# Split values as the stationary side in three attention branches, and a new order of branch C, of the start and of the last projection

## The chip, the core and the metric

The kernel runs as one program on one core of a Trainium2 chip. TensorE (PE in the profile) multiplies 128x128 blocks: a weight load (PEld) puts a stationary block into the array, and a matmul streams moving columns past it into PSUM. VectorE (DVE), ScalarE (ACT) and GpSimd (POOL) work element by element. Each engine runs its own list of instructions in order, and engines wait for each other by semaphores. The metric is device microseconds of one launch, the median of the runs.

## What is computed

Two layers, each a set of five attention branches (four heads each, 512 tokens, model width 1024) with gates, an output projection and a layer norm:

```python
def hybrid_layer(x, mem, ...):
    pr = split_projection(x @ w_in)
    o_a = dsa_attention(aq, ak, av, iq, ik, pr['i_w'])     # top 128 keys of each query, by index scores
    o_b = moba_attention(bq, bk, bv)                       # block-sparse, causal
    o_c = diff_attention(cq, ck, cv, lam)                  # (softmax1 - lam * softmax2) v
    o_d = mla_attention(qn, qr, kn, kr, v)                 # 96-wide keys from latents
    o_e = memory_attention(eq, mk, mv)                     # 256 memory tokens
    # each o_*: times silu(z), @ w_branch, times sigmoid(g); summed; @ w_out
    return layer_norm(alpha * x + out)

def mla_attention(qn, qr, kn, kr, v):
    s = (einsum('bqhd,bkhd->bhqk', qnb, kn) + einsum('bqhr,bkr->bhqk', qrb, kr)) * scale
    p = softmax(where(causal, s, -inf))
    return einsum('bhqk,bkhd->bqhd', p, v)
```

## The kernel before

**Products.** Each large product is made of three passes over operands split in a head and a rest (`product3`: head by head, head by rest, rest by head). The weights come by DMA in units (`WEIGHTS`): SyncE loads a unit, ACT copies its head (`split`, L1031), POOL subtracts for the rest (L721), and PE uses it in groups. A group `("grp", c, u, t)` is unit u of chunk c for token tile t: six matmuls with 512 moving columns (296 in chunk IX). A gate chunk (`gE0`, ...) has a fifth group per unit, t = 4, that projects a branch's output into bank U.

**The plan.** `plan()` writes one list, `PLAN`, for all engines: the groups in order, and after each group the smaller steps that `spread` puts between two places (`PLACES`) in equal shares of the groups' width. Every engine walks the same list, does its part of each step, and skips the rest. So what stands early in the list is early on every engine.

**Attention of A, B, D and E** (`att_steps`). Unit u = 4j + t is head j, query tile t, with (t + 1) x 128 keys (256 in E). Its steps are S (scores on PE into bank S; the mask and the row maximum on DVE, L1412; the exponential on ACT, L1114), two units later T (PE transposes the probabilities into bank TP, L962; ACT copies them to `PT`, L1120), and one more unit later V (PE, L977): f32 matmuls with a 128x128 block of `PT` stationary and 64 columns of values moving, t + 1 of them. Bank TP is free for the next T when ACT has copied it. After a head's last V, `fo` and `fin` (DVE) divide by the row sums and multiply by the gate z, and `yj` transposes the result and splits it for the branch's projection. `ev` and `er` copy and split the transposed queries and keys of a head (ACT, DVE) before its scores.

**Branch C** (`diff_steps`) has two score maps per unit; W (DVE, L1464 to L1467) joins them before T. Its keys and queries stand in the product banks G2 and G3, and its steps lie between (gA0,0,0) and (D0,3,2). W stands one half step before T, and `ev` of a map does queries and keys in one step.

**Start and end.** At the start the residual's four token tiles are normed (`ln0`), transposed and split (`xj`); the first groups go through units 0 and 1 of chunk IX, tile by tile. At the end of a layer chunk O1 runs units 0 and 1 over all tiles and then units 2 and 3 in pairs, tile by tile; `l1` and `l2` norm a finished tile (DVE, ACT, then POOL L677, then the store), and stand at the last groups.

## Time and profile before

| | us |
|---|---|
| median of 3 runs | 1382.11 |
| lowest and highest | 1380.39, 1382.39 |
| the profiled execution | 1384.15 |
| its span (first to last instruction) | 1382.5 |
| PE busy in it | 1328.0 (96%) |
| weight loads (PEld) busy | 1130.7 (82%) |
| DVE, ACT, POOL busy | 661.8, 653.3, 669.9 (48%, 47%, 48%) |

Busy time is a union of overlapping instructions, so a PE that is always busy may still be set by the pace of its matmuls. That pace is read from the starts of neighbouring rows in the timeline. A mean duration of a matmul is longer than its share of the engine.

### The profile page before, as it was taken

Reading aid. Unit: us, or ns where it says so; the run is one execution under the profiler, and the core shown is the slowest. Engines: PE = TensorE matmul, PEld = TensorE weight load, DVE = VectorE, ACT = ScalarE, POOL = GpSimd, SP = SyncE. Lnnn points to the kernel's source line nnn. Section 1 sums busy time; section 2 is a strip of 40 time slices with the busy share of each in tenths; the row PEclk is TensorE's granted clock in tenths of the full one; section 3 lists DMA queues with packets and bytes.
Section 4 is the critical chain, followed back from the end, with each engine's and each line's share of the span. In section 5 each row is a group of like instructions: output and inputs, shape, how many; then the busy total and the mean of one; then the engine's idle time right before and its main releaser. Section 6 shows DMA issues by size and latency. Waiting matters only on the chain.

```text
span 1382.5 us, 19021 instructions
## 1 busy us (share of the span) xinstructions
PE 1328.0 (96%) x6872; PEld 1130.7 (82%) x6872; DVE 661.8 (48%) x1609; ACT 653.3 (47%) x1296; POOL 669.9 (48%) x850
## 2 busy tenths in 40 slices
PE   6999999999988999999999999999999899999995
PEld 5888878888877898888888888888888779888884
DVE  4646696433155753213265668753322665432044
ACT  4455345454275664423245543555434665643232
POOL 3543453255563444467464435334446434645764
PEclk9899999999998999999999999999999999999998
DMA  7322242231331143232413223223123213323221
GB/s 258 114 77 62 81 114 58 67 88 47 103 95 37 37 123 107 58 107 77 140 49 106 68 71 106 81 58 85 53 74 111 59 33 86 95 65 100 84 77 61
DMA packets 147052, 116.47 MB, mean 84 GB/s; under 512 B 5520, under 2 KB 131856, under 8 KB 146704
## 3 DMA queue, kind: packets, MB, share of 16 engines
q1 hardware_dynamic: 146816, 114.22, 27.8%
q8 instruction: 55, 0.90, 0.3%
q10 hardware_dynamic: 144, 1.05, 0.2%
q14 instruction: 37, 0.30, 0.1%
HBM read 112.10 MB, written 3.15 MB: 83 GB/s over the span
## 4 chain that ended last, share of the span: by engine, by line
PE 79%; DVE 12%; ACT 4%; issue 2%; POOL 1%; DMA 1%; SPq 0%; POOLq 0%; DVEq 0%; ACTq 0%
PE product L737 19%; PE product L738 18%; PE product L739 18%; PE context L977 5%; PE scores L949 3%; PE transposed L962 3%; PE branch_product L737 2%; PE branch_product L739 2%; PE branch_product L738 2%; DVE index_scores L1389 2%; DVE top_eight L1395 1%; DMA residual<-in_x_dram 1%; ACT score_operands L1001 1%; POOL residual L677 1%; DVE vector_scratch L1214 1%
## 5 line engine op out<-in xcount | busy, mean ns | idle before, releaser
L721 POOL TENSOR_TENSOR weights_rest<-raw_weights,weights_head 128x320 fp32r<-128x320 f32 (+3 forms) x672 | 540.1, 836 | 376.8 <-ACT weights_head L1001 376.8
L737 PE MATMUL product<-weights_head,stationary_head 128*128 128x512 f32 (+3 forms) x768 | 291.4, 379 | 7.8 <-POOL weights_rest L721 7.6
L1001 ACT ACTIVATE weights_head<-raw_weights 128x1280 fp32r<-128x1280 f32 (+4 forms) x178 | 198.3, 1115 | 200.3 <-PE product L739 153.5
L739 PE MATMUL product<-weights_head,stationary_rest 128*128 128x512 f32 (+3 forms) x768 | 285.6, 372 | 0.0
L738 PE MATMUL product<-weights_rest,stationary_head 128*128 128x512 f32 (+3 forms) x768 | 285.4, 372 | 0.0
L737 PE MATMUL product<-stationary_head,weights_head 128*128 128x512 f32 x640 | 263.5, 412 | 0.0
L738 PE MATMUL product<-stationary_rest,weights_head 128*128 128x512 f32 x640 | 252.6, 395 | 0.0
L739 PE MATMUL product<-stationary_head,weights_rest 128*128 128x512 f32 x640 | 252.1, 394 | 0.0
L704 POOL TENSOR_TENSOR merged<-merged,activated 128x256 f32<-128x256 f32 x128 | 93.0, 748 | 291.4 <-DVE activated L1533 291.2
L737 PEld LDWEIGHTS product<-weights_head,stationary_head 128*128 128x128 f32 x768 | 145.7, 190 | 29.8 <-POOL weights_rest L721 8.4
L739 PEld LDWEIGHTS product<-weights_head,stationary_rest 128*128 128x128 f32 x768 | 145.4, 189 | 23.7
L738 PEld LDWEIGHTS product<-weights_rest,stationary_head 128*128 128x128 f32 x768 | 145.9, 190 | 20.2
L1114 ACT ACTIVATE probabilities<-probabilities,negated_maxima 128x256 f32<-128x256 f32 (+3 forms) x160 | 86.3, 540 | 155.4 <-DVE negated_maxima L1412 154.4
L739 PEld LDWEIGHTS product<-stationary_head,weights_rest 128*128 128x128 f32 x640 | 121.5, 190 | 27.5
L737 PEld LDWEIGHTS product<-stationary_head,weights_head 128*128 128x128 f32 x640 | 121.8, 190 | 20.8
L738 PEld LDWEIGHTS product<-stationary_rest,weights_head 128*128 128x128 f32 x640 | 122.1, 191 | 19.3
L1533 DVE SCALAR_TENSOR_TENSOR activated<-activated,branch_product 128x512 f32<-128x512 f32 x64 | 44.0, 687 | 154.5 <-PE branch_product L739 149.6
L1412 DVE CUSTOM_DVE_ANT_0 probabilities<-scores,consts_sb 128x256 f32<-128x256 f32 (+3 forms) x136 | 60.4, 444 | 110.8 <-PE scores L949 110.6
L1175 ACT ACTIVATE activated<-product 128x512 f32<-128x512 f32 x80 | 47.7, 596 | 131.4 <-PE product L739 130.5
L977 PEld LDWEIGHTS context<-values_and_gates,probabilities_T 128*128 128x128 f32 x640 | 89.8, 190 | 9.9 <-issue 1.4
L1001 ACT ACTIVATE probabilities_T<-transposed 128x256 f32<-128x256 f32 (+3 forms) x160 | 67.2, 420 | 55.3 <-PE transposed L962 54.0
L949 PE MATMUL scores<-score_operands 128*128 128x256 f32 (+7 forms) x288 | 77.7, 324 | 10.3 <-DVE score_operands L1350 6.1
(200 smaller groups left out, 1812.5 us busy)
## 6 DMA issues: line engine op xcount, KB each, us to landing
raw_weights<-in_w_in_dram SPq DMA_DIRECT2D x104, 512.0 KB, 3.7
raw_weights<-in_w_in_dram SPq DMA_DIRECT2D x72, 256.0 KB, 2.9
raw_weights<-in_w_branch_dram SPq DMA_DIRECT2D x80, 128.0 KB, 3.7
raw_weights<-in_w_out_dram SPq DMA_DIRECT2D x16, 512.0 KB, 3.6
merged<-in_w_mem_kv_dram SPq DMA_DIRECT2D x8, 512.0 KB, 7.3
raw_weights<-in_w_in_dram SPq DMA_DIRECT2D x8, 416.0 KB, 3.1
raw_weights<-in_w_in_dram SPq DMA_DIRECT2D x8, 296.0 KB, 3.8
residual<-in_x_dram SPq DMA_DIRECT2D x4, 512.0 KB, 11.4
```

The source lines that it names most:

```text
L704: ins = nc.gpsimd.tensor_tensor(m[:, part], m[:, part], TH[:, s, part], ALU.add)
L721: ins = nc.gpsimd.tensor_tensor(WL[:, sw, part], RAW[:, sr, part], WH[:, sw, part].bitcast(F32), ALU.subtract)
L737: nc.tensor.matmul(dst, sh, mh, start=start, stop=False)
L738: nc.tensor.matmul(dst, sh, ml, start=False, stop=False)
L739: return nc.tensor.matmul(dst, sl, mh, start=False, stop=stop)
L949: last = nc.tensor.matmul(S[:, 0:w], lhs, rhs, start=i == 0, stop=i == len(passes) - 1)
L977: last = nc.tensor.matmul(O[:, 0:BW][:, t * HD:(t + 1) * HD], PT[:, i * P:(i + 1) * P], v, start=i == 0, stop=i == w // P - 1)
L1001: return nc.scalar.activation(dst, src, ACT.Copy, scale=scale)
L1114: nc.scalar.activation(p, p, ACT.Exp, bias=NMX[:, m:m + 1], scale=-1.0, accum_out=RS[:, j % 2, 2 * t + u % 2 if b == "C" else t:(2 * t + u ...
L1175: nc.scalar.activation(TH[:, s, :], G[u % 2][:], ACT.Tanh, scale=0.5).then_inc(act_out.sem, act_out.step((c, u)))
L1412: nc.vector.tensor_tensor_reduce(probs(b, u)[:, 0:w], S[:, 0:w], bias, -SCALE[b], -TAKEN, ALU.add, ALU.min, NMX[:, u % 4:u % 4 + 1]).then_ ...
L1533: nc.vector.scalar_tensor_tensor(out=TH[:, s, :], in0=TH[:, s, :], scalar=1.0, in1=U[:], op0=ALU.add, op1=ALU.mult).then_inc(used.sem, not ...
```

## The change

Three things change together.

**Branches A, B and D** (`WIDE`). ACT copies the transposed probabilities as a head (fp32r, now a step of T), and a new step `pr` subtracts on DVE for the rest; both hold two query tiles side by side. A step `vs` splits a head's values into one 128-column block, head beside rest. V now exists for odd units alone: the split values are stationary, and 256 or 128 columns of probabilities move, head and rest, four matmuls for t = 1 and eight for t = 3. The output stands transposed in bank O, its two halves are added (`fo` on ACT, `fa` on DVE), and the gate z is divided by the row sums (`fin`), transposed (`zj`) and multiplied in. Bank TP is free only when `pr` is done.

**Branch C** starts at (C1,0,2), with its first head's queries and keys in banks U and O, and ends at (D0,3,1). W stands two half steps before T; `ev` and `er` handle one operand each.

**Start and end.** In chunk IX tiles 0 and 1 go through units 0 to 2 first. The splits of units 0 and 1 stand before the work on tile 3, the split of unit 2 behind it, and tile 3 of the input is loaded later. In chunk O1 each tile is finished in turn, and `l1`, `l2` of a tile stand one or two groups behind it. The early split of the next layer's first unit (`ahead`) goes.

```diff
+WIDE = "ABD"
...
+def wide_steps(b):
+    if b == "D":
+        out = [[("qt", b, 0)], [("ev", b, 0)], [("er", b, 0), ("qt", b, 1)], [("ev", b, 1)], [("er", b, 1)], [("vs", b, 0)]]
+    else:
+        out = [[("qt", b, 0)], [("ev", b, 0), ("er", b, 0)], [("ev", b, 1), ("er", b, 1)], [("vs", b, 0)]]
+    for i in range(UNITS + LAG_V + 1):
+        first, second = [], []
+        u = i - LAG_V
+        if 0 <= u < UNITS and u % 2 == 1:
+            first.append(("V", b, u))
+        if u >= NT and u % NT == 0:
+            first.append(("fa", b, u // NT - 1))
+        if 0 <= i - LAG_T < UNITS:
+            first.append(("T", b, i - LAG_T))
+            second.append(("pr", b, i - LAG_T))
+        if i < UNITS:
+            second.append(("S", b, i))
+        if i in (4, 8):
+            second += prep_steps(b, 1 + i // 4)
+        if i in (5, 9):
+            first.append(("er", b, 1 + i // 4))
+        if 0 <= u < UNITS and u % NT == NT - 1:
+            j = u // NT
+            second += [("fo", b, j)] + ([("vs", b, j + 1)] if j + 1 < NH else []) + [("fin", b, j)]
+        if i == 12:
+            second.append(("zj", b, 0))
+        if u == UNITS:
+            second.append(("zj", b, 1))
+        out += [first, second]
+    return out
...
 def diff_steps():
-    out = [[("qt", "C", 0)], [("ev", "C", 0, 0)], [("er", "C", 0, 0), ("ev", "C", 0, 1)], [("er", "C", 0, 1)], []]
-    late = []
+    out = [[("qt", "C", 0)]] + [[] for _ in range(5)]
+    early = {}
+    for j in range(NH):
+        for n in range(4):
+            m, part = divmod(n, 2)
+            at = {0: n - 5, 1: n}.get(j, 2 * (4 * j - 3) + 1 + n)
+            early.setdefault(at, []).append(("ev", "C", j, m, part))
+            early.setdefault(at + 1, []).insert(0, ("er", "C", j, m, part))
+    for n in range(5):
+        out[1 + n] += early.get(n - 5, [])
     for i in range(UNITS + 3):
-        first, second, third = [], [], []
+        first, second = [], []
         if 0 <= i - 3 < UNITS:
             first.append(("V", "C", i - 3))
+            if (i - 3) % NT == NT - 1:
+                first.append(("fo", "C", (i - 3) // NT))
+                second.append(("fin", "C", (i - 3) // NT))
         if 0 <= i - 2 < UNITS:
             first.append(("T", "C", i - 2))
         if i < UNITS:
             first.append(("S", "C", 2 * i))
-            second.append(("S", "C", 2 * i + 1))
+            second.insert(0, ("S", "C", 2 * i + 1))
         if 0 <= i - 1 < UNITS:
-            second.insert(0, ("W", i - 1))
-        second += late
-        late = []
-        if i >= 3 and (i - 3) % NT == NT - 1:
-            first.insert(1, ("fo", "C", (i - 3) // NT))
-            third.append(("fin", "C", (i - 3) // NT))
+            first.append(("W", i - 1))
         if i == 4:
-            third.append(("qt", "C", 1))
-        j, m = divmod(i + 3, 4)
-        if j < NH and m < 2 and i < UNITS:
-            third.append(("ev", "C", j, m))
-            late = [("er", "C", j, m)]
-        out += [first, second + third]
+            second.append(("qt", "C", 1))
+        out += [first + early.get(2 * i, []), second + early.get(2 * i + 1, [])]
...
-    ("lambda", ("gB1", 3, 3), ("C0", 0, 2), 0.0),
-    ("C attention", ("gA0", 0, 0), ("D0", 3, 2), 0.0),
+    ("lambda", ("gB0", 2, 0), ("gB0", 2, 0), 0.0),
+    ("C attention", ("C1", 0, 2), ("D0", 3, 1), 0.0),
...
-        pairs = {"IX": (0,), "O1": (2,)}.get(c, ())
-        for u in range(units(c)):
-            if u in pairs:
-                groups += [(c, u + i, t) for t in range(NT) for i in range(2)]
-            elif u - 1 not in pairs:
-                groups += [(c, u, t) for t in range(parts(c))]
+        order = [(u, t) for u in range(units(c)) for t in range(parts(c))]
+        if c == "IX":
+            order = [(u, t) for t in range(2) for u in range(3)] + [(u, t) for u in range(3) for t in (2, 3)] + [(3, t) for t in range(NT)]
+        elif c == "O1":
+            order = [(0, t) for t in range(NT)] + [(1, 0), (1, 1), (2, 0), (3, 0), (2, 1), (3, 1)] + [(u, t) for t in (2, 3) for u in range(1, 4)]
+        groups += [(c, u, t) for u, t in order]
...
-    start = [("ln0", 0), ("ln0", 1), ("mkv", 0), ("ln0", 2), ("xj", 0, 0), ("xj", 0, 1), ("ln0", 3), splits[0], ("mkv", 1),
-             ("xj", 1, 0), ("xj", 1, 1), ("ln0", 4), splits[1], splits[2]]
...
+    start = [("ln0", 0), ("ln0", 1), ("mkv", 0), ("ln0", 2), ("xj", 0, 0), ("xj", 0, 1), splits[0], splits[1], ("mkv", 1),
+             ("xj", 1, 0), ("xj", 1, 1), ("ln0", 3), splits[2], ("ln0", 4)]
+    extra[at[(ORDER[0], 1, 1)]] += [("xj", 2, 0), ("xj", 2, 1)]
+    extra[at[(ORDER[0], 2, 1)]] += [("xj", 3, 0), ("xj", 3, 1)]
...
-    extra[at[("O1", 2, 1)]] += [("ahead",) + WEIGHTS[0]]
-    extra[at[("O1", 3, 1)]] += [("l1", 0)]
-    extra[at[("O1", 3, 2)]] += [("l1", 1), ("l2", 0)]
-    extra[at[("O1", 3, 3)]] += [("l1", 2), ("l2", 1), ("l1", 3), ("l2", 2), ("l2", 3)]
+    for t in range(NT - 1):
+        i, j = {0: (("O1", 2, 1), ("O1", 3, 1))}.get(t, (("O1", 1, t + 1), ("O1", 2, t + 1)))
+        extra[at[i]].append(("l1", t))
+        extra[at[j]].append(("l2", t))
+    extra[at[("O1", 3, 3)]] += [("l1", 3), ("l2", 3)]
...
+        def wide(b):
+            if b == "D":
+                ph, pl = KLZ[:].rearrange("p a n -> p (a n)"), PL[:]
+            else:
+                ph, pl = (TL[:, a:a + 2, :].rearrange("p a n -> p (a n)") for a in (4, 6))
+            return [x.rearrange("p (i n) -> p i n", i=NT) for x in (ph, pl)] + [TL[:, 8, :].rearrange("p (i c d) -> p i c d", i=NT, c=2)]
+        def y_rows(k):
+            return PT if k == 0 else DS
...
-            load_x(3)
             load_mk(0, 3)
             for L in range(DEPTH):
                 new_layer([*raw, ln_in], L)
                 for i, item in enumerate(LOADS):
+                    if L == 0 and i == 2:
+                        load_x(3)
...
-                        freed["TP"] = (moved, L, step)
+                        freed["TP"] = (rest, L, ("pr", b, u)) if b in WIDE else (moved, L, step)
+                    elif kind == "V" and step[1] in WIDE:
+                        _, b, u = step
+                        j, t = divmod(u, NT)
+                        ph, pl, vs = wide(b)
+                        if t == 1:
+                            claim("O")
+                            pe.wait_ge(rest.sem, rest.at(L, ("vs", b, j)))
+                        pe.wait_ge(rest.sem, rest.at(L, ("pr", b, u)))
+                        blocks = [(0, ph), (t, ph), (t, pl)] + [(i, p) for i in range(1, t) for p in (ph, pl)]
+                        blocks.insert(3 if t == 1 else 1, (0, pl))
+                        for n, (i, p) in enumerate(blocks):
+                            at = P if i == t else 0
+                            last = nc.tensor.matmul(O[:, (t - 1) * P + at:(t + 1) * P], vs[:, i].rearrange("p c d -> p (c d)"),
+                                                    p[:, i, at:2 * P], start=n == 0, stop=n == len(blocks) - 1)
+                        last.then_inc(v_done.sem, v_done.step((b, u)))
+                        if t == NT - 1:
+                            freed["O"] = (summed, L, (b, j))
...
+                    elif kind == "vs":
+                        _, b, j = step
+                        if j > 0:
+                            act.wait_ge(v_done.sem, v_done.at(L, (b, NT * j - 1)))
+                        else:
+                            act.wait_ge(copied.sem, copied.at(L, ("dk" if b == "D" else b + "1", NT - 1)))
+                        copy(wide(b)[2][:, :, j % 2, :], VZ[:, vz(b), :, j * HD:(j + 1) * HD]).then_inc(moved.sem, moved.step(step))
+                    elif kind == "fo" and step[1] in WIDE:
+                        _, b, j = step
+                        r, o = rows(j)
+                        act.wait_ge(v_done.sem, v_done.at(L, (b, NT * j + NT - 1)))
+                        copy(y_rows(j // 2)[r, :], O[o, :]).then_inc(moved.sem, moved.step(step))
...
-                        copy(PT[:, 0:w], TP[:, 0:w]).then_inc(moved.sem, moved.step(step))
+                        if b in WIDE:
+                            half = slice(t % 2 * P, (t % 2 + 1) * P)
+                            copy(wide(b)[0][:, 0:t + 1, half], TP[:, 0:w].rearrange("p (i n) -> p i n", n=P)).then_inc(moved.sem, moved.step(step))
+                        else:
+                            copy(PT[:, 0:w], TP[:, 0:w]).then_inc(moved.sem, moved.step(step))
...
+                    elif kind == "vs":
+                        _, b, j = step
+                        v, vs = VZ[:, vz(b), :, j * HD:(j + 1) * HD], wide(b)[2]
+                        dve.wait_ge(moved.sem, moved.at(L, step))
+                        nc.vector.tensor_tensor(vs[:, :, 1 - j % 2, :], v, vs[:, :, j % 2, :].bitcast(F32),
+                                                ALU.subtract).then_inc(rest.sem, note(rest, step))
+                    elif kind == "pr":
+                        _, b, u = step
+                        t, _, w = unit(b, u)
+                        ph, pl, _ = wide(b)
+                        half = slice(t % 2 * P, (t % 2 + 1) * P)
+                        dve.wait_ge(moved.sem, moved.at(L, ("T", b, u)))
+                        nc.vector.tensor_tensor(pl[:, 0:t + 1, half], TP[:, 0:w].rearrange("p (i n) -> p i n", n=P),
+                                                ph[:, 0:t + 1, half].bitcast(F32), ALU.subtract).then_inc(rest.sem, note(rest, step))
+                    elif kind == "fa":
+                        _, b, j = step
+                        r, _ = rows(j)
+                        y = y_rows(j // 2)
+                        dve.wait_ge(moved.sem, moved.at(L, ("fo", b, j)))
+                        nc.vector.tensor_tensor(y[r, :], O[r, :], y[r, :], ALU.add).then_inc(summed.sem, note(summed, (b, j)))
...
```

On PE, in branch B's first head, the rows are the transposed probabilities (L962, L1030), the context products of the last query tile (L977, L1047) and the scores. Before:

```order
L949 MATMUL scores<-key_rests,score_operands 128x128
L977 MATMUL context<-values_and_gates,probabilities_T 128x64 x3
L962 MATMUL transposed<-consts_sb,probabilities 128x128 x4
L737 MATMUL product<-stationary_head,weights_head 128x512
```

Now:

```order
L1017 MATMUL scores<-key_rests,score_operands 128x256
L793 MATMUL product<-stationary_head,weights_head 128x512
...
L1047 MATMUL context<-score_operands 128x256 x2
L1047 MATMUL context<-score_operands 128x128 x2
L1047 MATMUL context<-score_operands 128x256 x4
L1030 MATMUL transposed<-consts_sb,probabilities 128x128
```

Before, each unit has its context product (three f32 matmuls here, each of which is two records in the trace). Now eight fp32r matmuls serve the two units t = 2 and t = 3.

On DVE, in branch C's first head, the rows are the mask and maximum of a score map (L1412, L1562), the joining of two maps (L1464 to L1467, L1614 to L1617) and the rests of the operands (L1348, L1350, L1501). Before:

```order
L1412 ISA index_scores,negated_maxima<-scores,consts_sb 128x512
L1412 ISA negated_maxima 128x1
L1533 SCALAR_TENSOR_TENSOR activated<-activated,branch_product 128x512
L1464 RECIPROCAL map_factors<-row_sums 128x1
L1465 SCALAR_TENSOR_TENSOR map_factors<-map_factors,lambdas,row_sums 128x1
L1467 SCALAR_TENSOR_TENSOR probabilities<-probabilities,map_factors 128x384
L1412 ISA index_scores,negated_maxima<-scores,consts_sb 128x512
```

Now:

```order
L1562 ISA index_scores,negated_maxima<-scores,consts_sb 128x512
L1562 ISA negated_maxima 128x1
L1614 RECIPROCAL map_factors<-row_sums 128x1
L1615 SCALAR_TENSOR_TENSOR map_factors<-map_factors,lambdas,row_sums 128x1
L1617 SCALAR_TENSOR_TENSOR probabilities<-probabilities,map_factors 128x384
L1683 SCALAR_TENSOR_TENSOR activated<-activated,branch_product 128x512
L1562 ISA index_scores,negated_maxima<-scores,consts_sb 128x512
```

The joining of unit 2 now stands ahead of the gate's multiplication (L1683), and directly behind the first mask of the unit after it.

On DVE, at the end of the program, the rows are the last tiles' residual, statistics and norm. Before:

```order
L1540 SCALAR_TENSOR_TENSOR residual<-product,residual 128x512
L1226 BN_STATS half_tile_stats<-residual 128x6
L1231 BN_AGGR norm_stats<-half_tile_stats 128x2
L1236 RECIPROCAL norm_stats<-deviations 128x1
L1237 SCALAR_TENSOR_TENSOR norm_stats<-norm_stats 128x1
L1243 TENSOR_TENSOR residual<-residual,values_and_gates 128x1024
L1283 SCALAR_TENSOR_TENSOR residual<-residual,norm_stats,values_and_gates 128x1024
L1243 TENSOR_TENSOR residual<-residual,values_and_gates 128x1024
L1292 RECIPROCAL norm_stats<-deviations 128x1
L1295 SCALAR_TENSOR_TENSOR residual<-residual,norm_stats,values_and_gates 128x512 x2
```

Now:

```order
L1351 TENSOR_TENSOR residual<-residual,values_and_gates 128x1024
L1690 SCALAR_TENSOR_TENSOR residual<-product,residual 128x512
L1334 BN_STATS half_tile_stats<-residual 128x6
L1339 BN_AGGR norm_stats<-half_tile_stats 128x2
L1391 SCALAR_TENSOR_TENSOR residual<-residual,norm_stats,values_and_gates 128x1024
L1400 RECIPROCAL norm_stats<-deviations 128x1
L1403 SCALAR_TENSOR_TENSOR residual<-residual,norm_stats,values_and_gates 128x512 x2
```

The two gains of earlier tiles (L1243) that stood behind the last tile's residual now stand ahead of it.

## Rows read from the trace of the kernel before

**Rows 1.** The page, part 1: busy us, share of the span, instructions.
```profile
PE 1328.0 (96%) x6872; PEld 1130.7 (82%) x6872; DVE 661.8 (48%) x1609; ACT 653.3 (47%) x1296; POOL 669.9 (48%) x850
```
**Rows 2.** Busy time by stretch: stretch, its length, engines, PEclk, DMA share, GB/s.
```profile
205.00:275.00 70.00, 68.76 (x385) 59.28 (x386) 39.65 (x99) 36.12 (x76) 23.38 (x28) 1.00 0.22 62
...
395.00:490.00 95.00, 86.94 (x443) 74.46 (x442) 57.04 (x148) 54.75 (x126) 40.09 (x51) 0.95 0.15 43
530.00:590.00 60.00, 60.00 (x344) 52.08 (x343) 17.41 (x49) 29.03 (x62) 27.66 (x35) 1.00 0.29 84
...
1068.00:1160.00 92.00, 83.90 (x428) 71.46 (x427) 56.49 (x146) 53.40 (x121) 38.71 (x49) 0.96 0.16 45
```
**Rows 3.** The waits of PE: total us, times, longest.
```profile
PE transposed L962 <- DVE probabilities L1467: 8.8, 10, 1.8
PE product L737 <- POOL weights_rest L721: 7.6, 3, 4.1
PE scores L949 <- DVE score_operands L1350: 6.1, 4, 1.5
```
**Rows 4.** The timeline of PE in branch A: start, duration, engine, line, names, count.
```profile
322.91 1.08 PEld L977 LDWEIGHTS context<-values_and_gates,probabilities_T 128*128 128x128 f32 x8
323.14 1.00 PE L977 MATMUL context<-values_and_gates,probabilities_T 128*128 128x64 f32 x8
...
323.97 0.28 PE L962 MATMUL transposed<-consts_sb,probabilities 128*128 128x128 f32 x1
```
**Rows 5.** The same, fp32r score matmuls of 256 and 128 columns in A and B.
```profile
321.52 0.28 PE L949 MATMUL scores<-score_operands 128*128 128x256 f32 x1
...
321.75 0.40 PE L737 MATMUL product<-stationary_head,weights_head 128*128 128x512 f32 x1
...
230.48 0.22 PE L949 MATMUL scores<-score_operands 128*128 128x128 f32 x1
...
230.66 0.83 PE L977 MATMUL context<-values_and_gates,probabilities_T 128*128 128x64 f32 x6
```
**Rows 6.** DVE, groups by line and shape: count, busy us, mean ns, idle before.
```profile
L1308 DVE TENSOR_TENSOR stationary_rest<-transposed,stationary_head 128x512 fp32r<-128x512 f32 x8 | 5.5, 690 | 19.8 <-ACT stationary_head L1001 19.8
```
**Rows 7.** The timeline of branch B: ACT's copy of the probabilities, and V.
```profile
233.55 0.60 ACT L1001 ACTIVATE probabilities_T<-transposed 128x512 f32<-128x512 f32 x1
...
234.78 1.00 PE L977 MATMUL context<-values_and_gates,probabilities_T 128*128 128x64 f32 x8
```
**Rows 8.** The timeline of branch C: DVE's joining and PE's wait.
```profile
412.27 1.05 DVE L1467 SCALAR_TENSOR_TENSOR probabilities<-probabilities,map_factors 128x384 f32<-128x384 f32 x1
...
413.46 0.52 PE L962 MATMUL transposed<-consts_sb,probabilities 128*128 128x128 f32 x3 [1.78 <-DVE probabilities L1467]
```
**Rows 9.** The timeline of the start.
```profile
26.01 1.28 DVE L1226 BATCH_NORM_STATS2 half_tile_stats<-residual 128x6 f32<-128x512 f32 x2
...
28.34 0.60 PE L856 MATMUL context<-consts_sb,residual 128*128 128x128 f32 x4
...
28.70 2.77 POOL L677 TENSOR_TENSOR residual<-residual,values_and_gates 128x256 f32<-128x256 f32 x4 [3.65 <-DVE residual L1243]
...
31.42 1.58 POOL L721 TENSOR_TENSOR weights_rest<-raw_weights,weights_head 128x320 fp32r<-128x320 f32 x2
...
33.06 0.61 PE L737 MATMUL product<-weights_head,stationary_head 128*128 128x296 f32 x1 [4.12 <-POOL weights_rest L721]
```
**Rows 10.** DVE's gains from 1357 us to the end, grouped by shape.
```profile
L1243 DVE TENSOR_TENSOR residual<-residual,values_and_gates 128x1024 f32<-128x1024 f32 x3 | 4.2, 1390 | 0.0
```
**Rows 11.** The timeline of the end.
```profile
1365.67 0.68 DVE L1540 SCALAR_TENSOR_TENSOR residual<-product,residual 128x512 f32<-128x512 f32 x1
1365.84 12.12 POOL L677 TENSOR_TENSOR residual<-residual,values_and_gates 128x256 f32<-128x256 f32 x12 [12.68 <-DVE residual L1243]
...
1372.51 2.15 DVE L1295 SCALAR_TENSOR_TENSOR residual<-residual,norm_stats,values_and_gates 128x512 f32<-128x512 f32 x2
...
1378.37 1.26 SPq L664 DMA_DIRECT2D out_dram<-residual  x2
```

133 lines of the change are left out of this document (85 added, 48 removed).

## The prediction

> **What bounds the kernel now.** I read the busy shares first: PE is busy for 1328.0 of 1382.5 us [rows 1]. Then the stretches, to see whether a full PE hides slack. In the stretch of branch D (530 to 590) PE is busy for all 60.00 us while DVE works 17.41 and ACT 29.03; in that of branch B 68.76 of 70.00, with DVE at 39.65. In the two stretches of branch C it is 86.94 of 95.00 and 83.90 of 92.00, and there the granted clock is 0.95 and 0.96 [rows 2]. Last the waits: most of what PE waits for is DVE in branch C (joined maps 8.8 us, rests of score operands 6.1 us) and POOL at the start (7.6 us) [rows 3]. So outside C and the two ends only less work on PE helps, inside C only shorter waits.
>
> **V of A, B and D.** In a head V was 1 + 2 + 3 + 4 = 10 f32 matmuls, and each stands as two records with a weight load of its own: four of them are eight records, and from their start to the next transpose are 0.83 us, so 0.104 us a record [rows 4]. A head costs 20 x 0.104 = 2.08 us. Now it is twelve fp32r matmuls, eight with 256 and four with 128 moving columns. The nearest rows are the score matmuls: two with 256 columns take 321.52 to 321.75, 0.115 us each; two with 128 take 230.48 to 230.66, 0.09 us each [rows 5]. That is 8 x 0.115 + 4 x 0.09 = 1.28 us. The difference is 0.80 us a head, for 4 heads, 3 branches and 2 layers 24 x 0.80 = 19.2 us. If a 128-column matmul costs a full 0.115 us, it is 16.8 us. All of it lies on PE in stretches where PE never rests, so I take 19.
>
> These eight records have one weight load each, 1.08 us in all, and start at the pace of the loads [rows 4]. The Trainium skill (FP8 and Floating Point Precision, section TensorE Precision Notes) says that true FP32 is four passes through the array. Priced by passed columns alone, an old block would be 4 x 64 columns and a head 2560, as many as the new twelve matmuls have, and the gain would be nothing. The trace speaks against pricing by columns here, since the loads set the pace.
>
> **What the new steps put beside it.** Per unit there is one subtraction on DVE from a PSUM bank. A 512-column one of that kind takes 0.69 us [rows 6]. PE's V now waits for ACT's copy and this, and the next T for it too, since the bank TP is held longer. In branch B the copy ends at 233.55 + 0.60 = 234.15 and V starts at 234.78 [rows 7]: a margin of 0.63 us, which 0.69 us and the queue of top-eight operations in front of it use up. In D (and in A, by the starts around 323 us) DVE has 40 us in 60 free [rows 2] and the plan leaves about the same two half steps, so I expect nothing there. In B some five odd units a layer are as tight; at 0.4 us each, both layers, that is 4 us. Bounds: 0 where the queue is empty, 12 us where one top-eight operation over 512 columns (about 0.7 us, taken as the 512-column row of [rows 6]) stands in front of each of the 16 V. The head's ends (`vs`, `fo`, `fa`, `zj`) have four half steps, some 6 us, until the next V or the projection wants them, and ACT and DVE need 0.6 + 0.7 us for each pair: nothing. With this cover gone each would cost its 1.3 us.
>
> **Branch C.** Idle PE in its stretches is 8.06 and 8.10 us; the reduced clock takes 0.05 x 95 = 4.8 and 0.04 x 92 = 3.7 us of full speed [rows 2]. The pool is 24.6 us. The waits come from W one half step before T: at 413.46 PE had waited 1.78 us, W ended at 412.27 + 1.05 = 413.32 [rows 8], and it had stood behind a gate multiplication. Now W stands two half steps before T and ahead of that multiplication, and the branch is spread over 68 groups where it had 55, so a half step grows from 1.28 to 1.55 groups: some 2.1 us of PE work where it was 1.75. From the last exponential W needs 1.7 to 2 us, and now has over 4. The rests of the keys come in four steps of one operand, each a half step apart, and end one half step before the scores. DVE has 57 us of work in 95, in the longer stretch about half. Late next is the first scores' key rest of each head, with one half step for 0.7 us. I take 22 of the 24.6 us, the clock's part with the waits', because it fell only beside them. Bounds: 11 (the waits halve, and the clock stays) and 25.
>
> **The end.** From the last tile's residual at 1365.67 to the end of its norm at 1372.51 + 2.15 = 1374.66 are 9.0 us [rows 11], and two gains of 1.39 us [rows 10] stand in it; both now lie before. One of them is still running when the last residual is ready, which costs 0.8 us. The norm ends at 1365.67 + 0.8 + 9.0 - 2.8 = 1372.7. Today the last stores wait until 1378.37, behind POOL's twelve pieces of 12.12 us [rows 11]. POOL now starts tile 2 at about 1366.4 and needs four pieces of 1.01 us, till 1370.5, with tiles 0 and 1 done before. So the stores follow at once, and 4.1 us after their issue the span ends, as now: 1376.9 instead of 1382.5, 5.6 us. Bounds 4 and 7. The split of unit 3 of O1 has three groups of 1.36 us less 0.1 us to spare: nothing.
>
> **The start.** Today PE waits 4.12 us for the first rest of weights, at 33.06 [rows 9]. The first split moves ahead of tile 3, so PE starts as its transposes end, about 29. But unit 2 is now wanted third, and its split stands behind tile 3, whose statistics stand on DVE behind the copies of tile 1: they begin at about 30, not at 26.01. From these statistics to POOL's first split are today 31.42 - 26.01 = 5.4 us, and the split takes 1.58 us [rows 9], so unit 2 is ready at 30.2 + 5.4 + 1.6 = 37.2, when PE has two groups done, as it has today at 37.5. The loads of tile 3 and of the weights change places under this. POOL's pieces may lengthen beside DVE's wide operations, so I take a loss of 1 us; bounds a gain of 3 and a loss of 4. In the second layer the same order costs and saves under 1 us.
>
> **The sum.** 19 + 22 + 5.6 - 4 - 1 = 41.6 us. The span goes from 1382.5 to 1340.9, the profiled execution from 1384.15 to 1342.6, which was 2 us above the median: the median goes from 1382.1 to 1340.5, so 1341.
>
> **Rivals.** 1. *DVE is late in B*: the twelve-microsecond bound is met, and small waits stand in A and D as well, 4 more. For it: the margin of 0.63 us; against it: B's DVE is free for 30 us in 70. It gives 1341 + 8 + 4 = 1353. Chance 0.16.
> 2. *C keeps half of its waits*, the clock with them: 1341 + 11 = 1352. For it: the operands of a head still end one half step before its scores. Chance 0.10.
> 3. *The V matmuls are no cheaper*, paced by the columns passed: 1341 + 19 = 1360. Against it are [rows 4, 5]. Chance 0.02. It is the case that the Trainium skill's rule above would give.
> 4. *A shared port.* POOL's pieces of 256 columns take 2.77 / 4 = 0.69 us at 28.70 and 12.12 / 12 = 1.01 us at the end [rows 9, 11], where wide DVE operations on two SBUF operands run beside them. The change adds such operations: 24 of `vs` at some 0.4 us and 12 splits of the branch output at 0.69, 18 us in all. If POOL's splits of weights stood still for them and PE felt a third, it would be 1341 + 6 = 1347. The Trainium skill (SBUF — State Buffer, section SBUF: two separate sides) states such a lock of the port that GpSimd shares with VectorE. Chance 0.04.
> 5. *All goes well*: no wait in B, a start that gains: 1341 - 4 - 4 = 1333. Chance 0.08.
> 6. *Slower*: the transposes wait for `pr` in every unit. There are 24 heads with four T and two V, 144 places, so 41.6 us are eaten at 0.29 us each. In B alone (48 places) one top-eight operation in front costs 34 us; if PE's clock in B then falls to the 0.9 to 0.95 that C has now, 140 us of B lose 7 to 14 us more, and with C's gain halved too, the kernel is at 1341 + 34 + 12 + 11 = 1398. It needs DVE full in B, which has 57% now and some 75% by my count after. Chance 0.04.
>
> The forecast itself, 1333 to 1349, has 0.56. The range must leave out no more than 2 in 10: 1329 to 1355, which takes in cases 1, 2, 4 and 5. About 0.2% is what a measurement can tell from no change: faster 0.95, same 0.01, slower 0.04.
>
> **What would show it.** In the profile after: context rows of A, B and D with 128x256 and 128x128 shapes and starts 0.115 and 0.09 us apart; no DVE joining among PE's waits, and a clock of 1.00 in C's stretches; a new wait of PE for DVE's rest of the probabilities in B, 2 to 6 us a layer, and near none in A and D; a wait of 4 to 6 us for POOL at about 32 us; last stores some 7 us after PE's last product. The forecast is wrong if the waits for that rest pass 12 us, or if the clock is below 1.00 in C or B.

## The result, and the profile after

| | before | changed |
|---|---|---|
| median, us | 1381.25 | 1422.38 |
| lowest and highest | 1379.29, 1382.39 | 1421.56, 1424.71 |
| span of the profiled execution | 1382.5 | 1423.1 |

The changed kernel takes 1.0302 times as long (95% interval 1.0283 to 1.0321): 41 us more, where 41 us less were forecast. The page's part 1, answering [rows 1]:

```profile
PE 1327.7 (93%) x6680; PEld 1115.5 (78%) x6680; DVE 735.9 (52%) x1741; ACT 673.9 (47%) x1344; POOL 673.8 (47%) x850
```

PE has 192 records fewer, 24 heads with twelve in the place of twenty, and DVE has 74 us more work. The waits of PE (total us, times, longest), answering [rows 3]:

```profile
PE context L1047 <- DVE score_operands L1435: 29.1, 21, 3.5
PE branch_product L949 <- DVE score_operands L1481: 11.7, 2, 5.9
PE product L793 <- POOL weights_rest L777: 10.4, 2, 8.9
PE scores L1017 <- DVE score_operands L1501: 6.7, 4, 1.9
PE context L1047 <- DVE probabilities_T_rest L1435: 6.4, 8, 1.1
PE scores L1017 <- DVE negated_maxima L1562: 6.4, 10, 2.1
```

The joining of the maps (8.8 us in [rows 3]) is gone. In its place stand 35.5 us of V waiting for `pr` (L1435, both of its rows), and two waits of 5.9 us for L1481, which is `ek`. Busy time in the stretches of B, A, C, D and of C in the second layer (columns as in [rows 2]):

```profile
203.00:290.00 87.00, 76.58 (x374) 62.65 (x373) 60.08 (x143) 40.35 (x83) 27.32 (x32) 0.94 0.22 60
290.00:370.00 80.00, 74.86 (x388) 61.51 (x387) 40.02 (x90) 42.43 (x87) 37.96 (x47) 1.00 0.23 67
416.00:515.00 99.00, 93.42 (x490) 81.46 (x491) 57.98 (x155) 57.10 (x132) 46.41 (x59) 0.98 0.19 56
536.00:620.00 84.00, 80.38 (x428) 66.77 (x427) 36.30 (x95) 41.16 (x86) 37.19 (x46) 1.00 0.30 86
1109.00:1209.00 100.00, 94.34 (x494) 82.01 (x493) 58.90 (x159) 57.48 (x134) 46.65 (x59) 0.98 0.20 56
```

B, which had 68.76 of 70.00 at a clock of 1.00 in [rows 2], has 76.58 of 87.00 at 0.94: it has become what C was. The same products run in both kernels, so their starts cut the two traces into like pieces. Each row is the time from the first product of one chunk to that of the next one named, layer 0 and layer 1, in us. The piece that begins with gE1 holds B's last three heads, and C's steps lie inside the piece that begins with C0:

| piece | before | changed | difference |
|---|---|---|---|
| start, up to A1 | 79.1 | 91.6 | +12.5 |
| A1 to gE1 (E, first head of B) | 146.0, 146.0 | 145.4, 145.5 | -0.6, -0.5 |
| gE1 to gB0 (rest of B) | 40.1, 40.1 | 53.5, 53.5 | +13.4, +13.4 |
| gB0 to C0 (A) | 75.7, 75.6 | 79.7, 79.6 | +4.0, +4.0 |
| C0 to gC0 (C) | 172.7, 171.8 | 166.0, 166.0 | -6.7, -5.8 |
| gC0 to gD0 (D) | 81.0, 81.0 | 83.4, 83.4 | +2.4, +2.4 |
| gD0 to O1 | 76.7, 76.7 | 76.2, 76.2 | -0.5, -0.5 |
| O1 to A1 of layer 1 | 80.9 | 89.3 | +8.4 |
| last O1 to the end | 39.0 | 33.9 | -5.1 |

So the three changed V cost 37.5 us (B, A, D and the two small pieces), the start and the layer's boundary 20.9, branch C gives 12.5 and the end 5.1.

**Where V waits.** The timeline of B at the end of its first head (start, duration, engine, line; idle time before and its releaser in brackets), PE:

```profile
232.04 1.20 PE L1047 MATMUL context<-score_operands 128*128 128x256 f32 x8 [0.17 <-DVE score_operands L1435]
233.08 0.27 PE L1030 MATMUL transposed<-consts_sb,probabilities 128*128 128x128 f32 x1
...
234.57 0.33 PE L1017 MATMUL scores<-score_operands 128*128 128x384 f32 x1
...
240.87 0.70 PE L1047 MATMUL context<-score_operands 128*128 128x256 f32 x4 [2.35 <-DVE score_operands L1435]
```

ACT: exponential (L1218), the output's copy `fo`, the values' copy of `vs`, and the copy of T:

```profile
235.71 0.62 ACT L1218 ACTIVATE probabilities<-probabilities,negated_maxima 128x384 f32<-128x384 f32 x1 [0.29 <-DVE negated_maxima L1562]
...
236.44 0.59 ACT L1088 ACTIVATE probabilities_T<-context 64x512 f32<-64x512 f32 x1
236.94 0.41 ACT L1088 ACTIVATE score_operands<-values_and_gates 128x256 fp32r<-128x256 f32 x1
237.37 0.38 ACT L1088 ACTIVATE score_operands<-transposed 128x256 fp32r<-128x256 f32 x1
```

DVE: `vs`, the division (`fin`), `fa`, a round of the top-eight selection, the gate's multiplication, and last `pr`:

```profile
237.38 0.42 DVE L1427 TENSOR_TENSOR score_operands<-values_and_gates,score_operands 128x256 fp32r<-128x256 f32 x1 [1.71 <-ACT score_operands L1088]
...
238.12 0.42 DVE L1460 TENSOR_TENSOR values_and_gates<-values_and_gates,reciprocals 128x256 f32<-128x256 f32 x1
238.47 0.67 DVE L1442 TENSOR_TENSOR probabilities_T<-context,probabilities_T 64x512 f32<-64x512 f32 x1
...
239.13 0.67 DVE L1539 MATCH_REPLACE8 index_scores<-top_eight,index_scores 128x512 f32<-128x512 f32 x1
239.73 0.67 DVE L1680 SCALAR_TENSOR_TENSOR merged<-activated,branch_product 128x512 f32<-128x512 f32 x1
240.32 0.41 DVE L1435 TENSOR_TENSOR score_operands<-transposed,score_operands 128x256 fp32r<-128x256 f32 x1
```

V of the first head was done at 233.08, but ACT reached the copies only after an exponential that had to wait for later scores. The copy of T, which `pr` reads, stood behind them too. DVE stood idle for 1.71 us, with five operations of 0.4 to 0.7 us (and two short ones) still to do before `pr`. The next two heads begin with waits of 3.46 and 2.38 us. In A the same places show 1.11, 2.11 and 1.19 us.

**The start.** PE, POOL and DVE:

```profile
40.77 0.61 PE L793 MATMUL product<-weights_head,stationary_head 128*128 128x296 f32 x1 [8.91 <-POOL weights_rest L777]
...
34.46 2.77 POOL L735 TENSOR_TENSOR residual<-residual,values_and_gates 128x256 f32<-128x256 f32 x4 [7.00 <-DVE residual L1351]
37.18 3.54 POOL L777 TENSOR_TENSOR weights_rest<-raw_weights,weights_head 128x320 fp32r<-128x320 f32 x2
...
31.77 1.28 DVE L1334 BATCH_NORM_STATS2 half_tile_stats<-residual 128x6 f32<-128x512 f32 x2
...
36.51 1.80 DVE L1351 TENSOR_TENSOR residual<-residual,values_and_gates 128x1024 f32<-128x1024 f32 x1 [1.31 <-ACT residual L1097]
38.34 1.76 DVE L1372 TENSOR_TENSOR residual<-residual,values_and_gates 128x1024 f32<-128x1024 f32 x1
```

PE has done two groups when it stands for 8.91 us. Some 27 us later, in chunk E, PE and DVE again:

```profile
67.59 0.42 PE L949 MATMUL branch_product<-consts_sb,merged 128*96 128x128 f32 x1 [5.86 <-DVE score_operands L1481]
67.67 0.78 PE L793 MATMUL product<-weights_head,stationary_head 128*128 128x512 f32 x1
...
55.90 0.64 DVE L1320 TENSOR_TENSOR vector_scratch<-staged_features,consts_sb 128x36 f32<-128x36 f32 x1 [6.04 <-ACT staged_features L1088]
...
64.49 1.41 DVE L1476 MEMSET score_operands<- 64x256 f32 x4
...
66.25 0.42 DVE L1481 TENSOR_TENSOR score_operands<-branch_product,score_operands 64x256 fp32r<-64x256 f32 x1
```

The first index transpose needs bank U, which holds memory keys until `ek` has read them. The change put `ek` behind (IX, 3, 1), and so behind the rotations of tiles 0 and 1 (L1320 to L1656), which keep DVE from 55.90 to 64.49. After the wait the granted clock is 0.50 from 67.6 to 72.0 (products of 0.63 to 0.78 us where 0.39 is usual). The second layer has the same wait, 5.86 us at 761.66.

### The profile page after: what moved, and what is told of

The parts are those of the page before. It is cut to its first block, busy times and chain, and to the rows that moved or that the text cites. A ratio compares the mean times of both kernels' runs of the same rounds, so it can differ in the third digit from the quotient of the medians.

```text
span 1423.1 us, 18843 instructions
## 1 busy us (share of the span) xinstructions
PE 1327.7 (93%) x6680; PEld 1115.5 (78%) x6680; DVE 735.9 (52%) x1741; ACT 673.9 (47%) x1344; POOL 673.8 (47%) x850
## 4 chain that ended last, share of the span: by engine, by line
PE 68%; DVE 20%; ACT 7%; issue 3%; POOL 1%; DMA 0%; DVEq 0%; ACTq 0%; SPq 0%
PE product L793 16%; PE product L795 16%; PE product L794 16%; PE context L1047 3%; PE scores L1017 2%; PE branch_product L793 2%; PE branch_product L795 2%; PE branch_product L794 2%; PE transposed L1030 2%; ACT score_operands L1088 2%; DVE index_scores L1539 2%; DVE probabilities L1562 2%; PE context L1064 1%; DVE top_eight L1545 1%; ACT probabilities L1218 1%
## 5 line engine op out<-in xcount | busy, mean ns | idle before, releaser
L777 POOL TENSOR_TENSOR weights_rest<-raw_weights,weights_head 128x320 fp32r<-128x320 f32 (+3 forms) x672 | 547.1, 845 | 414.0 <-ACT weights_head L1088 413.7
L1218 ACT ACTIVATE probabilities<-probabilities,negated_maxima 128x256 f32<-128x256 f32 (+3 forms) x160 | 86.6, 541 | 192.8 <-DVE negated_maxima L1562 190.8
L1683 DVE SCALAR_TENSOR_TENSOR activated<-activated,branch_product 128x512 f32<-128x512 f32 x64 | 43.9, 686 | 132.5 <-PE branch_product L795 128.4
L1562 DVE CUSTOM_DVE_ANT_0 probabilities<-scores,consts_sb 128x256 f32<-128x256 f32 (+3 forms) x136 | 60.0, 442 | 49.3 <-PE scores L1017 49.0
L1017 PEld LDWEIGHTS scores<-score_operands 96*128 96x128 f32 (+1 forms) x288 | 52.5, 190 | 28.1 <-DVE negated_maxima L1562 19.7
L793 PE MATMUL branch_product<-branch_out_T_head,weights_head 128*128 128x512 f32 x160 | 66.1, 413 | 0.0
```

What stands on the lines that cost most here:

```text
L777: ins = nc.gpsimd.tensor_tensor(WL[:, sw, part], RAW[:, sr, part], WH[:, sw, part].bitcast(F32), ALU.subtract)
L793: nc.tensor.matmul(dst, sh, mh, start=start, stop=False)
L1017: last = nc.tensor.matmul(S[:, 0:w], lhs, rhs, start=i == 0, stop=i == len(passes) - 1)
L1218: nc.scalar.activation(p, p, ACT.Exp, bias=NMX[:, m:m + 1], scale=-1.0, accum_out=RS[:, j % 2, 2 * t + u % 2 if b == "C" else t:(2 * t + u ...
L1562: nc.vector.tensor_tensor_reduce(probs(b, u)[:, 0:w], S[:, 0:w], bias, -SCALE[b], -TAKEN, ALU.add, ALU.min, NMX[:, u % 4:u % 4 + 1]).then_ ...
L1683: nc.vector.scalar_tensor_tensor(out=TH[:, s, :], in0=TH[:, s, :], scalar=1.0, in1=U[:], op0=ALU.add, op1=ALU.mult).then_inc(used.sem, not ...
```

## The experiments

Each is an edit of the changed kernel; medians are compared with 1422.4 us of the changed kernel and with the kernel before, run beside each (1381.6 to 1381.9).

**Old V.**

```diff
-WIDE = "ABD"
+WIDE = ""
```

> The changed kernel with the old V in A, B and D (branch C, the start and the end stay changed). Theory, read from the starts of the same product groups in the two traces: after the change B's stretch is 12.9 and 13.0 us longer, A's 4.0 and 3.9, D's 1.8 and 1.8, so the new V costs 37.4 us of 1422.4 and this kernel takes 1385, 4 us more than before. Rival 1: the loss sits in the other two parts, and V brings its gain: then this kernel is at or above 1422. Rival 2: taking V back also gives the clock and the queues of C and the start room: below 1378.

Measured: 1388.57 us (ratio to before 1.0054, 1.0039 to 1.0069). The new V costs 34 us. B's, A's and D's pieces are again 40.1, 75.7 and 81.0 us, as before to 0.1 us; the start, the boundary and C stay within 1.1 us of the changed kernel's. Neither rival stands. The median is 3.6 us above the sum; the profiled span, 1386.7, is 1.0 us above what the pieces give (1423.1 - 37.4).

**`ek` early.**

```diff
-    extra[at[(ORDER[0], 3, 1)]].append(("ek",))
+    extra[at[(ORDER[0], 1, 2)]].append(("ek",))
```

> The changed kernel with one step moved: ek (copies of the memory keys out of banks U and S, on ACT and DVE) stands behind group (IX, 1, 2), the ninth of the chunk's sixteen, and no longer behind (IX, 3, 1), where it stood behind the rotations of two tiles on DVE. Theory: PE's two waits of 5.86 us for line L1481 (at 67.6 and 761.7 us) go, and with each some 2 us of half clock behind it: 8.2 + 7.7 = 15.9 us less, 1406 to 1408. Rival: PE then waits nearly as long for the index transposes' own data, since the rotations themselves are late: at most 4 us less, 1418 or more.

Measured: 1406.88 us, 15.5 less. Both waits for L1481 are gone, and the pieces up to A1 are 83.5 us (91.6) and 82.2 us (89.3). The rival falls.

**Old start.**

```diff
-            order = [(u, t) for t in range(2) for u in range(3)] + [(u, t) for u in range(3) for t in (2, 3)] + [(3, t) for t in range(NT)]
+            order = [(u, t) for t in range(NT) for u in range(2)] + [(u, t) for u in (2, 3) for t in range(NT)]
...
-                    if L == 0 and i == 2:
-                        load_x(3)
```

with `splits`, `xj`, `ek` and the load of tile 3 where they were.

> The changed kernel with the start of before: the order of chunk IX's groups, the places of the splits, of xj and ek, and of the load of input tile 3 (the early split of the next layer stays away). Theory: the start's stretch up to chunk A1 is 12.5 us longer than before, and that of the second layer 8.4; all of it comes back, 1401.5. If ek alone is the cause (the run with ek early), this is within 5 us of that run. Rival: without the early split the second layer waits for it and keeps 4 us or more of its loss: 1405 or more.

Measured: 1404.14 us, between the theory (1401.5) and its rival (1405 or more). The start takes 77.3 us, 1.8 less than before, and the piece across the boundary 82.9 us (80.9 before, 89.3 changed): the second layer keeps 2 us, not the rival's 4. Whether they are the missing early split or the new order of O1, no run tells. Most of the loss of the start and boundary was `ek`. In layer 0 the new order of groups, splits and loads cost 83.5 - 77.3 = 6.2 us beside it, or 83.5 - 79.1 = 4.4 against the kernel before; no run tells where the 1.8 us between these two come from.

**The split of unit 2 ahead of tile 3**, with `ek` early:

```diff
-             ("xj", 1, 0), ("xj", 1, 1), ("ln0", 3), splits[2], ("ln0", 4)]
+             ("xj", 1, 0), ("xj", 1, 1), splits[2], ("ln0", 3), ("ln0", 4)]
```

> The kernel with ek early (1406.9 us), and the split of unit 2 of chunk IX ahead of the work on input tile 3. Theory: POOL's 3.5 us split at 37.18 us, which PE awaited for 8.9 us, is done before 29; the wait and the half clock behind it go, though PE then waits 2 to 3 us for tile 3: 6 to 8 us less, 1399 to 1401. Rival: tile 3 is what bounds the start in either order: at most 2 us less, 1405 or more.

Measured: 1403.42 us (1399.90 to 1404.21), 3.5 less by the medians, which is less than the theory asked for. In the profiled execution, the fastest of the four, the start takes 76.8 us, 6.7 less than with `ek` early alone and 2.3 less than before. Beside the run with the old start (77.3) the new order of groups is then worth 0.5 us: no loss, and hardly a gain. The two POOL pieces of this split:

```profile
31.54 1.57 POOL L777 TENSOR_TENSOR weights_rest<-raw_weights,weights_head 128x320 fp32r<-128x320 f32 x2 [4.32 <-ACT weights_head L1088]
```

In the changed kernel the same two pieces took 3.54 us, beside DVE's two additions over 128x1024.

**A second buffer for the split values**, in A and B, with `vs` behind the first V of the head before:

```diff
-                        if j > 0:
-                            act.wait_ge(v_done.sem, v_done.at(L, (b, NT * j - 1)))
+                        if j > 0 and b == "D":
+                            act.wait_ge(v_done.sem, v_done.at(L, (b, NT * j - 1)))
+                        elif j > 1:
+                            act.wait_ge(v_done.sem, v_done.at(L, (b, NT * (j - 1) - 1)))
...
+        if b != "D" and u % NT == 1 and 0 <= u < UNITS - NT:
+            second.append(("vs", b, u // NT + 1))
```

Heads 1 and 3 use `PL`, which is free outside D.

> The changed kernel with two buffers for the split values of A and B: the split of a head's values stands right behind the first V of the head before, and waits for no output. D is as changed. Theory (head of line): at a head's end DVE stood idle 1.7 us for ACT's copy of the values, which stands behind an exponential and the copy of the output, and pr of the next head stood behind that; PE's waits at the first V of heads 1 to 3 (2.35, 3.46 and 2.38 us in B, 1.11, 2.11 and 1.19 in A, each layer) fall to a third, and the half clock behind two of them in B goes: 20 us less or more, 1402 or less. Rival (DVE is full: top-eight, gate and mask in front of pr): DVE is only filled in another order, at most 5 us less, 1417 or more.

Measured: 1413.59 us, 8.8 less: between the two theories. The waits at the first V of a head became smaller, but new ones stand at the second V, where `vs` now stood ahead of `pr`, with a clock fall behind the largest:

```profile
239.34 0.70 PE L1049 MATMUL context<-score_operands,probabilities_T_rest 128*128 128x256 f32 x4 [0.96 <-DVE score_operands L1439]
248.37 2.08 PE L1049 MATMUL context<-score_operands,probabilities_T_rest 128*128 128x256 f32 x8 [2.94 <-DVE score_operands L1439]
```

**Without the selection of tile 3.**

```diff
-        "top of tile 3": tops[3] + [[("KB",)]]
+        "top of tile 3": tops[3][:2] + [[("KB",)]]
```

> The changed kernel with only the first of the sixteen rounds of top-eight for query tile 3 (30 DVE operations of 0.68 us each and their value loads are left out of B's stretch in each layer; the selection is incomplete). Theory (DVE is full in B: rounds stand ahead of pr): B's stretch falls from 53.5 us to 43 or less, 1422 less 20 or more, 1402 or less; with the runs on V this tells how much of B's loss is queueing. Rival (the chain at a head's end, scores, mask, exponential, copy of the output, copy and rest of the values, then pr, holds V by itself): B stays above 49, at most 9 us less, 1413 or more.

Measured: 1412.96 us, 9.4 less, with B at 49.3 and 48.3 us: 20 us of DVE's work gone from B in each layer, and 4 to 5 us less. It lies at the rival's edge (B above 49, 1413 or more), far from the theory: queueing behind the rounds is a part, and not the largest.

**Without the rests of the probabilities.**

```diff
-                        pe.wait_ge(rest.sem, rest.at(L, ("pr", b, u)))
+                        pe.wait_ge(moved.sem, moved.at(L, ("T", b, u)))
+                        pl = ph
```

with `pr` skipped on DVE, and bank TP free for the next T when ACT has copied it, as with the old V.

> The changed kernel without the rests of the probabilities: DVE skips pr, and V takes the head in its place (same number and shape of matmuls; the rest's part of the result is left out). The values' split vs stays. Theory (pr and the queue in front of it are what V waits for): B's stretch falls from 53.5 to 38 or 39 us a layer, A's from 79.7 to 74, D's from 83.4 to 79, all of it 45 to 52 us, 1371 to 1377; it also shows V's price without waits, by starts 1.4 to 1.6 us a head against 2.0 before. Rival (vs and the output bank at the head's end hold V, not pr): half of it stays, 1395 or more.

Measured: 1394.60 us, 27.8 less, on the rival's side (1395 or more; the theory had 1371 to 1377). B is at 45.7 and 44.1 us, A at 75.2, D at 81.0. What V waits for in this kernel:

```profile
PE context L1048 <- DVE probabilities_T L1444: 9.8, 10, 2.2
...
PE context L1048 <- DVE vector_scratch L1444: 4.0, 4, 1.3
```

L1444 is `fa`, the addition that frees the output bank O. It stands on DVE behind the same `vs` and `fin`. This trace also prices V: by the starts of its records, in D's piece, the new V takes 1.38 us in 128-column and 4.63 us in 256-column records, 6.0 us for four heads, where the old one took 8.04. That is 0.51 us a head less, not 0.80.

**The order at a head's end, and the second buffer.** To `split2`, both are done at once: `fo` directly behind V and ahead of the scores' exponential, `fin` behind `pr` of the next head's second unit, and `vs` of A and B in the second buffer behind `pr` of unit 4j + 3:

```diff
-            second += [("fo", b, j)] + ([("vs", b, j + 1)] if j + 1 < NH else []) + [("fin", b, j)]
+            second.insert(0, ("fo", b, j))
+            if j + 1 < NH and b == "D":
+                second.append(("vs", b, j + 1))
+        if u >= NT and u % NT == 0:
+            second.append(("fin", b, u // NT - 1))
+        if b != "D" and u % NT == 2 and 0 <= u < UNITS - NT:
+            second.append(("vs", b, u // NT + 1))
```

> The kernel split2 (1403.4 us), and for the new V: a second buffer for the split values of A and B, their split behind pr of unit 4j + 3 (not ahead of it); ACT's copy of the output directly behind the last V and ahead of the next exponential; the gate's division (fin) behind pr of the next head's second unit. Theory (three things hold V at a head's end: the values' chain, what stands ahead of pr on DVE, and the output bank that fa frees late): each is moved off, B's stretch falls from 53 to 43 or less and A's from 79.7 to 76, 28 us less, 1376. It stays above the kernel with old V and this start (1366.3). Rival (DVE's work itself is too much for B, in whatever order): B stays above 47, 1388 or more.

Measured: 1361.18 us (ratio to before 0.9850, 0.9834 to 0.9866), 42.2 less than `split2`. The theory's side, and more than it asked for. Its last sentence did not hold: this kernel is 5.2 us faster than the one with the old V and the same start (1366.3), not slower. B is at 40.9 us, A at 74.6, D at 80.3. The waits for `pr`, 35.5 us before, are now 6.7:

```profile
PE context L1053 <- DVE score_operands L1443: 5.1, 10, 0.9
...
PE context L1053 <- DVE probabilities_T_rest L1443: 1.6, 2, 0.8
```

At the same place as above ACT copies the output ahead of the exponential, and DVE's `pr` ends before PE wants it (the V row has no wait):

```profile
219.58 0.59 ACT L1094 ACTIVATE probabilities_T<-context 64x512 f32<-64x512 f32 x1
220.07 0.60 ACT L1226 ACTIVATE probabilities<-probabilities,negated_maxima 128x384 f32<-128x384 f32 x1
...
222.06 0.41 DVE L1443 TENSOR_TENSOR score_operands<-transposed,score_operands 128x256 fp32r<-128x256 f32 x1
...
222.97 0.62 PE L1053 MATMUL context<-score_operands,probabilities_T_rest 128*128 128x256 f32 x4
```

**The same without `pr`.**

> The same, and pr is left out on DVE (V takes the head in place of the rest; the rest's part of the result is missing). Theory: with the output bank freed early too, nothing holds V, and B's and A's stretches are 2.1 us below those of before (four heads by 0.52 us, V's price as the starts in the run without pr show it): B 38, A 73.6, and the kernel at 1357 to 1361, 5 to 9 us below the one with old V. Rival: the output bank still holds the second V of each head, B 42 or more, 1366 or more.

Measured: 1351.03 us, 6 us beyond the theory's 1357. B is at 38.7 us, A at 72.8, D at 79.1, and V of A, B and D has no wait left. So `pr` costs 10 us even in the better order, and the new V without it would give 15.3 us against the old V (1366.3, below). Here V is also cheaper by the starts of its records: 1.37 and 4.31 us in D's piece, 1.42 us a head, 0.59 less than the old. The first 256-column matmul of a V takes 0.11 us where PE had not waited, as in this V (0.46 us to the transposes), and 0.19 to 0.22 right behind a wait, as at 240.87 in the changed kernel (0.54 us):

```profile
235.12 0.62 PE L1054 MATMUL context<-score_operands 128*128 128x256 f32 x4
235.58 0.49 PE L1036 MATMUL transposed<-consts_sb,probabilities 128*128 128x128 f32 x3
```

**Each part alone**, on `split2`. Order alone (`fo` and the next head's `vs` directly behind V, `fin` late, one buffer):

> split2 (1403.4 us) with the order alone: fo and the next head's vs directly behind the last V, ahead of pr, of the scores and so of ACT's exponential, and fin behind pr of the next head's second unit; one buffer for the split values, as in the changed kernel. Theory 1 (ACT's exponential, on which copy of the output and of the values queue behind, is what holds the head's end): most of the 42 us that wide_tuned took over split2 comes, 1372 or less. Theory 2 (the single buffer holds it, since vs still needs the last V's end): 1385 or more.

Measured: 1386.01 us, 17.4 less. V now waits 7.4 us for `pr` (36.4 in `split2`), but T, whose bank `pr` frees, waits 17.2 us for it, 14.3 of them in A and B. B's piece is 45.3 and 43.9 us, D's 82.0; A keeps 79.8, and the piece A1 to gE1 grows by 2.3 and 3.7 us.

```profile
PE transposed L1034 <- DVE score_operands L1439: 14.3, 8, 2.1
```

In this order `vs`, which still waits for the last V, stands directly ahead of `pr` on DVE.

The second buffer alone (`fo` and `fin` as in the changed kernel):

> split2 with the second buffer alone: vs of A and B behind pr of unit 4j + 3, waiting for no output; fo and fin as in the changed kernel (behind the scores and ACT's exponential, fin and fa ahead of pr). Theory 1 (the order of fo and fin): at most 12 us less than split2, 1391 or more. Theory 2 (the buffer): 1376 or less.

Measured: 1374.33 us (ratio to before 0.9950, 0.9937 to 0.9963), 29.1 less. B's piece is 43.7 us, A's 75.2; D, which has no second buffer, keeps 83.4. Neither expectation for the first theory holds; the second theory's numbers, for the order (1385 or more) and for the buffer (1376 or less), both do, the first by 1 us. The sum 17.4 + 29.1 = 46.5 is near the 42.2 of both together.

But this run changed two things: `vs` no longer waits for the last V, and it stands behind `pr` of the second V. The run with `vs` early had the same buffer with `vs` one unit earlier, ahead of that `pr`, and was left with 48.1 and 45.9 us in B and 80.0 in A, so the place is worth 2 to 4 us a layer in B and all that A gains. In D, which keeps one buffer, the piece falls to 82.0 us with `vs` ahead of `pr` (order alone) and to 80.3 with `vs` behind it (both at once). What the runs show is thus that `vs` ahead of `pr` holds V, and the next T; a `vs` that waits for the last V has little other room. A and B with one buffer and `vs` behind `pr` were not tried.

**Old V with the mended start** (`WIDE = ""`, `ek` early, the split of unit 2 ahead of tile 3):

> Old V in all branches, the changed C and end, ek early, and the split of unit 2 of chunk IX ahead of the work on input tile 3. Theory (parts add): before 1381.6, C 12 to 15 us less, the end 5 less, the start and the boundary about as before: 1363 to 1367. Rival: the parts share a clock or a queue and do not add: 1372 or more.

Measured: 1366.34 us (0.9894, 0.9872 to 0.9917), in the theory's range. The parts add.

**Branch C's operands earlier**, on this kernel:

```diff
-            at = {0: n - 5, 1: n}.get(j, 2 * (4 * j - 3) + 1 + n)
+            at = {0: n - 5, 1: n}.get(j, 2 * (4 * j - 3) + n)
```

> The kernel best3 (old V, changed C and end, mended start; 1366.3 us), with the copies and rests of branch C's operands for heads 1 to 3 one half step earlier. Theory: PE's four waits of 1.5 to 1.9 us for line L1501 (6.7 us in all) go; as no half clock stood behind them, 5 to 7 us less, 1360 to 1361. Rival: DVE has no room there, and the steps only push the masks and joinings: no change, 1365 or more.

Measured: 1360.90 us, 5.4 less; no wait for L1501 is left, and the piece C0 to gC0 is 164.2 and 162.6 us, against 172.7 and 171.8 before.

**All together**: `wide_tuned` with C's operands earlier.

> wide_tuned (1361.2 us) and branch C's operand steps one half step earlier as in c_early, which took 5.4 us. Theory (the branches are apart and add): 1355 to 1357. Rival: they share something: 1359 or more.

Measured: 1355.22 us (0.9813, 0.9786 to 0.9839). As expected, the branches add. This beats both kernels, the one before by 1.9%.

## Why the prediction was wrong

**V's price** ("8 x 0.115 + 4 x 0.09 = 1.28 us", 19 us in all). Mis-sized. The old V was right to 4% (2.0 us a head against 2.08). The new takes 1.42 us a head where it never waits, and 1.50 in D's piece of the first run without `pr`, not 1.28. Its 256-column matmuls start 0.117 to 0.120 us apart within a run and the 128-column ones 0.085, as forecast, but a 256-column one that follows a 128-column one takes 0.17, and the first of a run 0.19 to 0.22 right behind a wait. The gain is 24 x 0.59 = 14 us by the records and 15.3 us by the run without `pr`, not 19. The shapes were right and the third rival (no cheaper) falls.

**The new steps.** Here the prediction failed. It looked at one step, `pr`, and at its ordinary place, and allowed 4 us in B with 12 as the bound. It is 35.5 us of waits, in all three branches. For the head's ends it said that `vs`, `fo` and `fa` "have four half steps, some 6 us, until the next V", and put nothing. But `fo` and `vs` stand between the last V and `pr` of the next head's second unit, in a chain over three engines (last V on PE, ACT behind an exponential, DVE), and `pr` stands behind `vs` on DVE's in-order list, though it needs nothing of it. The runs show it: with a second buffer, `vs` behind `pr` and `fo` ahead of the exponential the waits fall to 6.7 us and the time by 42 us, while all but one of sixteen selection rounds removed from the queue give 9. The cover that was named ("with this cover gone each would cost its 1.3 us") was also mis-priced: what is lost is the wait of everything behind.

In A and D "I expect nothing there" was wrong: their pieces are 4.0 and 2.4 us a layer longer, where V's price promised 3.2 us less. The same edits take it back (74.6 and 80.3 us). That DVE is free for half the time (40.02 us of 80.00 busy in A, 36.30 of 84.00 in D) does not help where the order binds it.

The sixth rival had the right side (1398 forecast, 1422 found), but the mechanism it named, transposes waiting for `pr` in every unit, is not what happened: they wait for `pr` for 0.2 us in all, and only with the order alone does that wait become large (17.2 us). Its clock term was right: B's clock fell to 0.94.

**Branch C** (22 us, bounds 11 and 25). Mis-sized. The joining's waits went, as forecast; 12.5 us came, near the second rival's 11. The prediction named what was late next, "the first scores' key rest of each head, with one half step for 0.7 us", and did not charge it: it is the row L1501, 6.7 us. One half step more gave 5.4 us. In the timeline DVE works without a gap before that wait:

```profile
453.49 0.68 DVE L1501 TENSOR_TENSOR score_operands<-product,score_operands 32x512 fp32r<-32x512 f32 x1
454.21 0.69 DVE L1562 CUSTOM_DVE_ANT_0 index_scores<-scores,consts_sb 128x512 f32<-128x512 f32 x1
...
454.94 0.69 DVE L1501 TENSOR_TENSOR score_operands<-product,score_operands 32x512 fp32r<-32x512 f32 x1
...
455.77 0.30 PE L1017 MATMUL scores<-score_operands 96*128 96x128 f32 x1 [1.52 <-DVE score_operands L1501]
```

A new wait came of the earlier start as well: masks of the first head stand on DVE behind the gates of chunk C1's tiles, which wait for ACT (2.09 us at 420.06). That it is the earlier start was argued from the timeline, not tried. The clock's part was right in direction: 0.98 in both stretches, not 1.00.

**The end** (5.6 us, bounds 4 and 7). Right in sum, 5.1 us, and partly by luck. The rows that answer [rows 11]:

```profile
1413.47 1.22 DVE L1351 TENSOR_TENSOR residual<-residual,values_and_gates 128x1024 f32<-128x1024 f32 x1 [1.31 <-ACT residual L1097]
1414.62 0.68 DVE L1690 SCALAR_TENSOR_TENSOR residual<-product,residual 128x512 f32<-128x512 f32 x1
...
1418.05 1.69 DVE L1403 SCALAR_TENSOR_TENSOR residual<-residual,norm_stats,values_and_gates 128x512 f32<-128x512 f32 x2
...
1414.78 3.75 POOL L735 TENSOR_TENSOR residual<-residual,values_and_gates 128x256 f32<-128x256 f32 x4 [1.95 <-DVE residual L1351]
```

The last product starts at 1411.10 and the last residual at 1414.62, 3.5 us later, where it was 0.64 in the kernel before (1365.03 and 1365.67): it stood behind tile 2's gain, which had itself waited 1.31 us for ACT. That is 2.9 us where 0.8 was allowed. In return its norm ends 5.1 us after it, at 1419.74, where 9.0 - 2.8 = 6.2 was forecast, and the span 3.3 us later, not 4.1.

**The start** (a loss of 1 us, bounds +3 and -4). Wrong, by two steps. The working followed the third split: statistics at "about 30", 5.4 us to POOL's split, 1.6 us for it. They began at 31.77, the split at 37.18 (5.41 us later), and took 3.54 us. So the chain was right and the split's duration was not. Then it counted two groups as done, "as it has today", and called the outcome 1 us; PE waited 8.91 us, and the order, the splits and the loads cost 4.4 us in layer 0 against the kernel before. The larger step was not there at all: `ek` is moved in the diff by five groups, and the prediction never asked what it is moved past. It is 15.5 us over both layers. So the second layer did not cost "under 1 us": its boundary is 8.4 us longer, 7.1 of them `ek`.

**The shared port** (0.04). Rival 4 had its place wrong. POOL's 576 pieces of 320 columns took 914 ns on average, 901 in the kernel before: 7.6 us in all, on an engine that waits most of the time. But its split at the start took 1.77 us a piece beside DVE's wide additions and 0.79 us in the run where it stood apart from them. The Trainium skill (SBUF — State Buffer, section SBUF: two separate sides) speaks of a lock on the port that GpSimd and VectorE share. This pair agrees in direction with that.

**The other signs.** No joining among the waits: right. A clock of 1.00 in C: 0.98. Waits for the rest of 2 to 6 us a layer in B and near none in A and D: wrong, and 35.5 us is past the 12 us that it gave as the sign of its failure. A wait of 4 to 6 us for POOL at about 32: 8.9 us, from 31.9.

## What to carry to other kernels

When a change adds a step to an engine's in-order list, ask what every later step on that list now waits for, not whether the engine has time: a step that waits for another engine holds all that stands behind it. A single buffer that the next group may refill only when the last one is read ties two groups together across engines; give it a second copy, put the refill behind the steps that the busy engine is waiting for, or price the whole chain. And in a diff that moves many steps, list each moved one with what it is moved past, the small ones too: one bookkeeping step moved by five groups cost as much here as the gain from V.

## What was not expected of the hardware

- The same two POOL subtractions of 128x320 and 128x272 took 3.54 us beside two DVE additions over 128x1024, and 1.57 us without them. The DVE additions took 1.80 and 1.76 us there, where such a one took 1.17 us at 33.21.
- The first 256-column matmul of a V takes 0.19 to 0.22 us from start to start right behind a wait of PE, and 0.11 us where PE had not waited (the medians of `tuned_no_pr`, where almost none waits). One behind a 128-column one takes 0.17 us, against 0.118 within the run. So a wait costs some 0.1 us more than its length, and prices from pairs within a run are too low for short runs.
- The waits of 8.91, 5.86 (twice), 3.48 and 3.46 us in the changed kernel each have a stretch of half clock behind them (after the last of these, at 257.64, the granted clock is 0.50 from 257 to 263, with products 0.43 us apart where 0.23 is usual). Of two nearly equal waits in B the one of 2.35 us at 240.87 had none (clock 1.00 from 235 to 245), and the one of 2.38 us at 275.55 had one (0.83 from 275 to 285). The same wait of 2.09 us in C had one in layer 0 (0.57 from 420 to 424) and none in layer 1 (1.00 from 1113 to 1118). The length of the last wait alone does not tell it.
